# The gate product of a recurrence moved from VectorE to GpSimd, with its split taken earlier and the projection behind it in one piece

## The reference

```python
def _rglru_branch(xb, yb, conv_w, conv_b, w_rg, b_rg, w_ig, b_ig, lru_lambda, w_o_lru):
    xc = conv_b + sum(xpad[:, k:k + s] * conv_w[k] for k in range(CONV_WIDTH))
    r = sigmoid(einsum('bsgi,gij->bsgj', xg, w_rg) + b_rg)
    ig = sigmoid(einsum('bsgi,gij->bsgj', xg, w_ig) + b_ig)
    log_a = -LRU_C * r * softplus(-lru_lambda)
    a = exp(log_a)
    gated_x = sqrt(-expm1(2.0 * log_a)) * (ig * xc)
    _, h = associative_scan(_lru_combine, (a, gated_x), axis=1)
    return (h * gelu(yb)) @ w_o_lru
```

## Time and profile before

| what | value |
|---|---|
| time, median of three runs | 2514.73 us (2510.97 to 2518.98) |
| the profiled execution's own time | 2510.97 us |
| its span | 2509.2 us |
| TensorE busy | 2348.1 us (94% of the span) |
| VectorE busy | 991.8 us (40%) |
| ScalarE busy | 859.5 us (34%) |
| GpSimd busy | 317.2 us (13%) |
| scans of the recurrence (L824) | 8 of 2.29 us, from 827.4 to 999.7 |
| products with the gate (L830) | 8 of 1.23 us |

### The profile page before, as it was taken

How to read it: one execution, slowest core, us unless ns; L and a number is a source line. 1 busy time by engine, 2 the same in 40 slices (tenths; PEclk the granted TensorE clock), 3 DMA queues, 4 the chain that set the end, 5 groups by cost and what they waited for, 6 DMA issues and landing times.

```text
span 2509.2 us, 25993 instructions
## 1 busy us (share of the span) xinstructions
PE 2348.1 (94%) x10629; PEld 1945.1 (78%) x10629; DVE 991.8 (40%) x1097; ACT 859.5 (34%) x1233; POOL 317.2 (13%) x364
## 2 busy tenths in 40 slices
PE   7999999999998999999996667789999999999997
PEld 6888888888786888888885555667888888888885
DVE  3334333433336564212125655365343233332333
ACT  3322233322224666212234454334332223222222
POOL 0000001200003211000123343223110000200001
PEclk9999999999999999999998898999999999999998
DMA  5333333343232121224101001255433422443221
GB/s 173 95 102 110 128 99 101 118 133 94 93 96 68 49 55 36 85 72 123 43 31 29 9 5 51 88 178 166 125 119 93 134 101 84 122 131 118 93 93 67
DMA packets 278016, 232.55 MB, mean 93 GB/s; under 512 B 22853, under 2 KB 250250, under 8 KB 277898
## 3 DMA queue, kind: packets, MB, share of 16 engines
q1 hardware_dynamic: 277898, 230.89, 29.8%
HBM read 209.36 MB, written 20.97 MB: 92 GB/s over the span
## 4 chain that ended last, share of the span: by engine, by line
PE 80%; DVE 7%; issue 6%; ACT 4%; POOL 3%; DMA 1%; SPq 0%; POOLq 0%; ACTq 0%; DVEq 0%
PE ps L85 26%; PE ps L87 26%; PE ps L86 26%; DVE a_pt L95 1%; DVE a_s L1432 1%; PE ps L1495 1%; PE ps L320 1%; ACT a_probs L1442 1%; POOL b_sum L1634 1%; POOL r_xc L844 1%; DVE r_xc L824 1%; DVE w_lo L95 1%; ACT a_pt L91 0%; POOL r_xc L841 0%; POOL x L287 0%
## 5 line engine op out<-in xcount | busy, mean ns | idle before, releaser
L85 PE MATMUL ps<-u_hi,w_hi 128*128 128x512 f32 x1920 | 750.4, 391 | 6.9 <-DVE w_lo L95 3.6
L87 PE MATMUL ps<-u_hi,w_lo 128*128 128x512 f32 x1920 | 748.3, 390 | 0.0
L86 PE MATMUL ps<-u_lo,w_hi 128*128 128x512 f32 x1920 | 748.3, 390 | 0.0
L95 DVE TENSOR_TENSOR w_lo<-w_raw,w_hi 128x1024 fp32r<-128x1024 f32 (+2 forms) x345 | 427.6, 1242 | 656.8 <-ACT w_hi L91 656.6
L91 ACT ACTIVATE w_hi<-w_raw 128x1024 fp32r<-128x1024 f32 (+2 forms) x345 | 355.3, 1033 | 480.1 <-PE ps L87 442.3
L85 PEld LDWEIGHTS ps<-u_hi,w_hi 128*128 128x128 f32 x1920 | 361.3, 188 | 83.0 <-issue 6.0
L87 PEld LDWEIGHTS ps<-u_hi,w_lo 128*128 128x128 f32 x1920 | 361.1, 188 | 75.4
L86 PEld LDWEIGHTS ps<-u_lo,w_hi 128*128 128x128 f32 x1920 | 361.3, 188 | 74.3
L85 PE MATMUL ps<-w_hi,hs 128*128 128x512 f32 x704 | 275.3, 391 | 12.9 <-DVE hs L95 9.6
L86 PE MATMUL ps<-w_lo,hs 128*128 128x512 f32 x704 | 274.6, 390 | 0.0
L87 PE MATMUL ps<-w_hi,hs 128*128 128x512 f32 x704 | 274.4, 390 | 0.0
(11 more groups left out here) (213 smaller groups left out, 2462.4 us busy)
## 6 DMA issues: line engine op xcount, KB each, us to landing
w_raw<-in_ffn_w_gate_dram SPq DMA_DIRECT2D x88, 512.0 KB, 3.8
w_raw<-in_ffn_w_up_dram SPq DMA_DIRECT2D x88, 512.0 KB, 3.7
w_raw<-in_ffn_w_down_dram SPq DMA_DIRECT2D x88, 512.0 KB, 3.4
w_raw<-in_w_in_dram SPq DMA_DIRECT2D x32, 512.0 KB, 3.8
w_raw<-in_w_out_dram SPq DMA_DIRECT2D x24, 512.0 KB, 3.5
x<-in_x_dram SPq DMA_DIRECT2D x16, 512.0 KB, 6.3
h_scratch<-x SPq DMA_DIRECT2D x16, 512.0 KB, 5.0
x<-h_scratch SPq DMA_DIRECT2D x16, 512.0 KB, 5.5
```

What stands on the lines that cost most here:

```text
L85: pe.matmul(out, lh, rh, start=start, stop=False)
L86: pe.matmul(out, lh, rl, start=False, stop=False)
L87: return pe.matmul(out, ll, rh, start=False, stop=stop)
L95: return nc.vector.tensor_tensor(lo, src, as_f32(hi), ALU.subtract)
```

## The change

Three edits:

1. The product with the gate leaves VectorE (`out` is gone) and is the third instruction of GpSimd's `products`, with the same waits.
2. On ScalarE `out_hi` of d stands ahead of the gelu of d + 1, where it stood behind it.
3. `branch_of(0)` and `branch_of(1)` wait for all eight splits before their first matmul; the first is no longer taken in two parts.

```diff
@@ Recurrence
-    def out(self, dve, d):
-        to = self.xc[:, d % 2, :]
-        dve.wait_ge(self.S["scan_done"], d + 1)
-        dve.wait_ge(self.S["gelu_done"], d + 1)
-        self.nc.vector.tensor_tensor(to, to, self.gate_y[:, :], ALU.mult).then_inc(self.S["out_done"], 1)
...
         self.nc.gpsimd.tensor_tensor(to, to, self.r[:, :], ALU.mult).then_inc(self.S["bx_done"], 1)
+        pool.wait_ge(self.S["scan_done"], d + 1)
+        pool.wait_ge(self.S["gelu_done"], d + 1)
+        self.nc.gpsimd.tensor_tensor(to, to, self.gate_y[:, :], ALU.mult).then_inc(self.S["out_done"], 1)
@@ LruMerge.branch_of
-        elif d == 0:
-            pe.wait_ge(self.rec.S["sig_r"], DK)
-            pe.wait_ge(self.rec.S["out_split"], DK - 1)
-        for blocks in (range(DK - 1), range(DK - 1, DK)) if d == 0 else (range(DK),):
-            if d < 2 and blocks[-1] == DK - 1:
-                pe.wait_ge(self.rec.S["out_split"], DK)
-            for hf in range(2):
-                for k in blocks:
...
+        else:
+            pe.wait_ge(self.rec.S["out_split"], DK)
+        for hf in range(2):
+            for k in range(DK):
...
@@ ScalarE's program
                     if d + 2 <= DK:
                         w.hi(act, (rec.n_y + [ring[1]])[d + 2])
+                    rec.out_hi(act, d)
                     if d + 1 < DK:
                         rec.gelu(act, d + 1)
-                    rec.out_hi(act, d)
@@ VectorE's program
                     rec.scan(dve, d)
-                    rec.out(dve, d)
                     if d + 2 <= DK:
                         w.lo(dve, (rec.n_y + [ring[1]])[d + 2])
```

More of the change, by code:

```diff
@@ L953, in branch_of @@
             pe.wait_ge(self.S["prod_done"], d - 1)
-        elif d == 0:
-            pe.wait_ge(self.rec.S["sig_r"], DK)
-            pe.wait_ge(self.rec.S["out_split"], DK - 1)
-        for blocks in (range(DK - 1), range(DK - 1, DK)) if d == 0 else (range(DK),):
-            if d < 2 and blocks[-1] == DK - 1:
-                pe.wait_ge(self.rec.S["out_split"], DK)
-            for hf in range(2):
-                for k in blocks:
-                    last = mm3(pe, c.ps[:, self.branch_bank(d) + hf, :], self.w.both(self.n_b[d], slice(k * P, (k + 1) * P)),
-                               tuple(x[:, k, half_of(hf)] for x in (self.rec.lru_hi, self.rec.lru_lo)), k == 0, k == DK - 1)
+        else:
+            pe.wait_ge(self.rec.S["out_split"], DK)
+        for hf in range(2):
+            for k in range(DK):
+                last = mm3(pe, c.ps[:, self.branch_bank(d) + hf, :], self.w.both(self.n_b[d], slice(k * P, (k + 1) * P)),
+                           tuple(x[:, k, half_of(hf)] for x in (self.rec.lru_hi, self.rec.lru_lo)), k == 0, k == DK - 1)
         last.then_inc(self.w.used, 1)
```

## The result

| | before | changed |
|---|---|---|
| median | 2512.99 us (4 runs, 2510.97 to 2518.98) | 2542.85 us (4 runs, 2539.04 to 2543.4) |
| profiled execution, span | 2509.2 us | 2536.7 us |
| TensorE busy | 2348.1 us | 2357.5 us |
| scans of the recurrence, first and last start | 827.4, 999.7 | 828.2, 1014.7 |

The ratio is 1.0111, 95% interval 1.0091 to 1.0133: slower by 1.1%, some 28 us by the ratio and 29.9 by the two medians. Forecast was 2540, range 2529 to 2549.

What follows compares the result with a forecast made beforehand. TensorE was taken as the bound, with VectorE's loop nearly level in the recurrence. Later scans 13.6, last product 1.25, unsplit branch 9.52 less 0.62 and clock 2.3 made 26.1 us, giving 2540 us, range 2529 to 2549.

Steps and rivals of the forecast that it cites:

- The two loops run nearly level: Recurrence passes before the change: VectorE's loop takes 25.23 us, TensorE's 24.48, so added time soon becomes TensorE time.
- The product takes 3.29 us beside w_lo: GpSimd's gate product, 2.40 us alone, takes 3.29 beside VectorE's w_lo; ScalarE has it 2.11 us later than before.
- lru_hi first gains nothing, because w_hi closes the pass: On ScalarE: VectorE's second w_lo still waits for w_hi, so each pass grows by 1.93 us to 27.16.
- The last pass hangs on the sigmoid, + 2.13: Without a convolution, the last pass waits on ScalarE's sigmoid, 2.13 us later: scan 7 comes 23.03 us after scan 6.
- The unsplit branch, + 9.52 and - 0.62: Merge: 42 more TensorE matmuls fall behind the last lru_lo, + 9.52 us; the later sigmoid wait goes, - 0.62.
- The low clock, + 2.3: After TensorE idles some 10 us before the first merge lru matmul, half-speed clock costs 2.3 us (bounds 0 and 2.3).
- Sum: Total added up to the merge: 13.6 + 1.25 + 9.52 - 0.62 + 2.3 = 26.1 us, expected to be handed on whole.
- no collision: Rival: w_lo does not hold GpSimd's product, so passes grow only 1.03 us; 2535 us, chance 0.20.
- the low clock costs in the passes: Rival: low clock after each 2.7 us gap costs 2 us in each of five passes; 2550 us, chance 0.08.
- handed back later: Rival: TensorE waits in the attention stage, some behind weight loads, absorb half the shift; 2527 us, chance 0.08.
- not slower: Rival: w_lo does not wait for w_hi, so the reorder shortens the loop and TensorE's waits go; 2513 us, chance 0.04.

Runs made afterwards that it cites:

- c_later_lo: The changed kernel with the w_lo after the scan moved behind lru_lo on VectorE, so nothing of VectorE runs beside the GpSimd product: 2537.5 us, ratio 1.0088.
- d_order: The kernel before with edit 2 alone (lru_hi ahead of the gelu on ScalarE): 2515.67 us, ratio 1.0004 to the kernel before.
- e_early: The changed kernel with one weight split (w_hi, w_lo) moved ahead of the waits for the product in passes 0 to 5: 2525.66 us, ratio 1.0039.
- a_split: The changed kernel with the split of branch 0 put back, so edits 1 and 2 alone: 2532.27 us, ratio 1.0065 to the kernel before.
- b_unsplit: The kernel before with edit 3 alone (branch 0 in one piece behind the last split): 2527.61 us, ratio 1.0052.
- f_early_split: As e_early but with branch 0 split as before, so edits 1 and 2 and the early weights: 2514.55 us, ratio 0.9997.
- h_early_order: The kernel before with edit 2 and the early weight split of e_early, product on VectorE, branch 0 split: 2515.47 us, ratio 0.9999.

## Why the prediction was right

- *The two loops run nearly level.* Right. The pass of the changed kernel is 27.23 us (27.16 predicted; the table load starts 1.08 us behind lru_hi and not 0.95), and TensorE waits from the third pass on, as said. Scan 7 is 14.1 us later, counted from scan 0, where 13.6 were predicted.
- *The product takes 3.29 us beside w_lo.* Right to the hundredth, because the earlier trace rows has the same pair, w_lo and a GpSimd instruction with two SBUF operands, in the same order of starts behind a VectorE instruction. (That one differs: a sum from PSUM there, the scan here.) c_later_lo shows the cause by taking w_lo away from beside the product.
- *lru_hi first gains nothing, because w_hi closes the pass.* Right: in the changed kernel the second w_lo waits 2.06 us for w_hi, d_order alone changes nothing that the time shows, and e_early, which moves that w_hi, takes 3 us out of every pass.
- *The last pass hangs on the sigmoid, + 2.13.* The last scan is 1014.66 - 991.59 = 23.07 behind the one before it (23.03 predicted), the product there 2.34 us alone.
- *The unsplit branch, + 9.52 and - 0.62.* With the low clock 11.2 were predicted (9.52 - 0.62 + 2.3). Added last, to edits 1 and 2, edit 3 costs 10.3 us in the traces and 10.6 in the times (a_split); alone it costs 11.2 and 12.9 (b_unsplit).
- *The low clock, + 2.3.* Mis-sized: 1.5 us behind the last wait of the changed kernel. The wait there was 8.28 us and not 10: behind the waits of 2.46, 2.47 and 2.48 us for the gelu the clock was low too (0.50 from 892 to 894), and the last of these, at 1000.82, slowed the second merge gate itself to 12.8 us from 10.9, so that TensorE came later to its wait. In the passes it cost nothing, as predicted: the wait that follows such a stretch is 0.96 or 0.89 us where the others are 2.46 to 2.48, so the 1.5 us lost are taken out of the next wait. The prediction had 2.7 in each.
- *Sum.* 26.1 predicted; at the next merge gate 25.6 measured after the 0.85 from ahead of the stage. That these are so close is in part luck: the passes came out 0.5 us longer and the clock 0.8 cheaper. The span has 27.5, of which 0.85 from ahead of the stage and 1.1 of clock in attention are no work of the edits and were not foreseen.

Of the rivals, "no collision" falls by the product's 3.29 us; "the low clock costs in the passes" by passes of 27.23; "handed back later" by the 26.3 us at both ends of the latents and the 27.5 of the span; "not slower" by the wait for w_hi, though e_early and f_early_split show that its mechanism is real once that w_hi stands elsewhere.

## What to carry to other kernels

When an instruction moves to another engine or ahead of another, look for the last wait of the loop on every engine, not for the operand that the move releases: here lru_lo came 2.2 us sooner and the loop only 0.1, since an unrelated weight split stood behind the same wait. A step that depends on nothing late (the w_hi of the next block) belongs in front of a wait, where it cost nothing that the times show (f_early_split); in its place behind the wait it turned a delay of 2.1 us, harmless otherwise, into 2 us a pass. And a wait that looks small in a trace can be small because the work was arranged around it: price the arrangement (42 matmuls in front of the wait) and not the wait.

## What the hardware showed

- After waits of the same length the clock behaved differently. In the changed kernel it stayed at 1.00 behind the wait of 1.93 us at 864.68, and fell to the lower level for some 3 us behind 2.46 us at 891.91. In a_split it fell behind a wait as short as the first, 1.96 us at the same place in the program (0.53 from 864.95 to 867):

```profile
864.95 0.65 PE L85 MATMUL ps<-u_hi,w_hi 128*128 128x512 f32 x1 [1.96 <-ACT r_gate_y L761]
```

- Nor does a longer wait cost more clock. The 48 matmuls behind the last lru_lo take 10.88 us at the full level. Behind a wait of 8.28 us (the changed kernel) they lost 1.5 us, behind 8.25 (e_early) 1.9, behind 9.85 (c_later_lo, 1016.98 to 1029.29) 1.4 and behind 9.64 (b_unsplit) 2.5. The same order of work costs between 1.4 and 2.5 us of clock, which a prediction can only give as a range.
- The hold between VectorE and GpSimd goes both ways in one pass of e_early: GpSimd's product takes 3.30 us for 2.39, and then two w_lo take 4.54 us for the 2.35 of h_early_order:

```profile
954.19 2.35 DVE L95 TENSOR_TENSOR w_lo<-w_raw,w_hi 128x1024 fp32r<-128x1024 f32 x2
```
